# State-space preparation in another order: rotation tables before output matrices, first four table pairs ahead of the kernel copies

## What is computed

```python
dt = exp(log_dt); a_bar = exp(lam * dt)              # 32 groups, 64 complex states each
b_bar = ((a_bar - 1.0) / lam)[..., None] * b
bu = einsum('bsgc,gpc->bsgp', u, b_bar)
states = scan over positions of s = a_bar * s + bu   # complex, diagonal
y = einsum('bsgp,gcp->bsgc', states, c).real + d_skip * u
```

## Time and profile before

| | |
|---|---|
| median of 3 runs | 3012.65 us (3012.24 to 3018.19) |
| profiled execution | 3006.3 us |
| its span | 3004.5 us |
| PE busy | 2803.8 us, 93% of the span |
| DVE busy | 1913.6 us, 64% |
| ACT busy | 1357.6 us, 45% |
| POOL busy | 936.6 us, 31% |

### The profile page before, as it was taken

One profiled execution on the slowest core, in us unless ns is written; L12 is line 12 of the kernel. 1 busy time (PEld: TensorE's weight loads), 2 busy tenths in 40 slices (PEclk: granted clock), 3 DMA queues, 4 the chain that ended last, 5 costly groups with the idle time before them and its releaser, 6 DMA issues. The chain is left out here.

```text
span 3004.5 us, 43240 instructions
## 1 busy us (share of the span) xinstructions
PE 2803.8 (93%) x14883; PEld 2367.3 (79%) x14883; DVE 1913.6 (64%) x2803; ACT 1357.6 (45%) x2268; POOL 936.6 (31%) x743
## 2 busy tenths in 40 slices
PE   6999967879999998997899989999999999999999
PEld 5888854669899897886788778887888787878777
DVE  5334338768778786545667675657555868686864
ACT  4222224657667675322344455556555424242321
POOL 0011100745455552320000032333323344444443
PEclk9999988989999999998999999999999999999999
DMA  5333345263422203344132334333544374756555
GB/s 169 92 87 81 99 125 71 55 189 72 95 57 57 61 22 102 105 147 161 36 119 105 117 104 136 103 108 130 179 139 140 102 167 100 170 95 154 119 111 88
DMA packets 296004, 328.21 MB, mean 109 GB/s; under 512 B 114584, under 2 KB 221088, under 8 KB 295584
## 3 DMA queue, kind: packets, MB, share of 16 engines
q1 hardware_dynamic: 276960, 291.96, 32.7%
q0 software_dynamic: 18432, 33.56, 7.9%
q10 hardware_dynamic: 464, 0.79, 0.1%
HBM read 206.57 MB, written 126.88 MB: 111 GB/s over the span
## 5 line engine op out<-in xcount | busy, mean ns | idle before, releaser
L3235 PE MATMUL f_ps_bank<-f_big,h_wv 128*128 128x512 f32 x1280 | 503.1, 393 | 25.6 <-DVE f_big L3081 20.3
L3236 PE MATMUL f_ps_bank<-f_big,h_wv 128*128 128x512 f32 x1280 | 500.0, 391 | 0.0
L3237 PE MATMUL f_ps_bank<-f_big,h_wv 128*128 128x512 f32 x1280 | 500.0, 391 | 0.0
L704 POOL TENSOR_TENSOR a_w<-a_on,a_left 128x640 f32<-128x640 f32 (+5 forms) x192 | 282.1, 1469 | 243.3 <-DVE a_left L756 108.9
L3077 DVE TENSOR_TENSOR h_wv<-h_w_raw,h_wv 128x512 fp32r<-128x512 f32 x189 | 241.9, 1280 | 155.1 <-ACT h_wv L2978 151.7
L2978 ACT ACTIVATE h_wv<-h_w_sum 128x512 fp32r<-128x512 f32 x252 | 158.9, 631 | 349.7 <-PE f_ps_bank L3237 342.2
L2919 POOL TENSOR_TENSOR h_w_sum<-h_w_raw 128x512 f32<-128x512 f32 x63 | 91.2, 1447 | 721.6 <-DMA h_w_raw<-in_w_up 441.8
L3235 PEld LDWEIGHTS f_ps_bank<-f_big,h_wv 128*128 128x128 f32 x1280 | 241.5, 189 | 83.5 <-issue 28.8
L3237 PEld LDWEIGHTS f_ps_bank<-f_big,h_wv 128*128 128x128 f32 x1280 | 241.4, 189 | 50.7
L3236 PEld LDWEIGHTS f_ps_bank<-f_big,h_wv 128*128 128x128 f32 x1280 | 241.7, 189 | 49.5
L846 PE MATMUL a_ps_y<-a_wt,a_v 128*96 128x128 f32 x2176 | 269.9, 273 | 3.3 <-DVE a_yt L779 3.3
(11 more groups left out here) (400 smaller groups left out, 6211.2 us busy)
## 6 DMA issues: line engine op xcount, KB each, us to landing
h_w_raw<-in_w_up SPq DMA_DIRECT2D x32, 1024.0 KB, 6.7
a<-h_xr SPq DMA_DIRECT2D x128, 256.0 KB, 3.4
h_w_raw<-a SPq DMA_DIRECT2D x32, 1024.0 KB, 5.1
out<-h_xr POOLq DMA_DIRECT2D x128, 256.0 KB, 4.0
h_raw<-in_w_down SPq DMA_DIRECT2D x32, 512.0 KB, 6.5
p_xt<-in_x SPq DMA_DIRECT2D x16, 512.0 KB, 4.5
p_raw<-in_w_in SPq DMA_DIRECT2D x16, 512.0 KB, 5.4
q<-p_raw SPq DMA_DIRECT2D x64, 128.0 KB, 2.5
```

Of the source, the lines that this page charges most:

```text
L704: pool.tensor_tensor(w[m % WS][:, 0:k1 - k0], on[m % ONS][:, 0:k1 - k0], left[a][i % 2][:, at + k0 + 1:at + k1 + 1], ALU.mult).then_inc(we ...
L3235: pe.matmul(o, wv(i, 0)[:, k, :], hv(i, 0)[:, k, :], start=(k == 0), stop=False)
L3236: pe.matmul(o, wv(i, 0)[:, k, :], hv(i, 1)[:, k, :], start=False, stop=False)
L3237: mm = pe.matmul(o, wv(i, 1)[:, k, :], hv(i, 0)[:, k, :], start=False, stop=(k == KH - 1))
```

## The change

On DVE the block of the output matrices is moved behind the low tables. On ACT, `parts` for pairs 0 to 3 is moved from behind the copies of the kernel and of `mat_out_j` to ahead of both. No instruction is added or taken away, apart from where they wait; the loops of PE, POOL and SP are as they were.

```diff
@@ ACT
             for n in range(G // 4):
                 copy_in(n)
+            act.wait_ge(low_ready, 1)
+            for p in range(4):
+                parts(p, 0)
+                parts(p, 1)
             for n in range(G // 4):
                 act.wait_ge(kern_made, n + 1)
                 act.activation(kern[:, 4 * n:4 * n + 4, :], y_ps[n % 2][0:C, :].rearrange("p (g s) -> p g s", g=4),
...
                                ACT.Copy).then_inc(crossed_copied, 1)
-            act.wait_ge(low_ready, 1)
-            for p in range(4):
-                parts(p, 0)
-                parts(p, 1)
             for p in range(1, PAIRS):
@@ DVE
             dve.sem_inc(keys_scaled, 1)
 
-            dve.wait_ge(in_rows, 1)
-            c_of = [cc[:, x, :].rearrange("p (g c) -> p g c", c=C) for x in range(2)]
-            above = pw[:, 1:SUB + 1, :, :]
-            both(dve.tensor_copy(mat_out[:, :, 0, :], c_of[0]),
-                 dve.tensor_tensor(mat_out[:, :, 1:, :], by_row(c_of[0]), by_power(above, 0), ALU.mult),
-                 dve.tensor_tensor(wide4, by_row(c_of[1]), by_power(above, 1), ALU.mult))
-            dve.tensor_tensor(mat_out[:, :, 1:, :], mat_out[:, :, 1:, :], wide4, ALU.add).then_inc(out_rows, 1)
-
             def normalise(v, n, shape):
...
-            dve.wait_ge(out_rows, 1)
             both(dve.tensor_copy(turn8[:, 0, :], num[:, 9, :]), dve.tensor_copy(turn8[:, 1, :], num[:, 6, :]))
...
             dve.engine_nop().then_inc(low_ready, 1)
+
+            dve.wait_ge(in_rows, 1)
+            c_of = [cc[:, x, :].rearrange("p (g c) -> p g c", c=C) for x in range(2)]
+            above = pw[:, 1:SUB + 1, :, :]
+            both(dve.tensor_copy(mat_out[:, :, 0, :], c_of[0]),
+                 dve.tensor_tensor(mat_out[:, :, 1:, :], by_row(c_of[0]), by_power(above, 0), ALU.mult),
+                 dve.tensor_tensor(wide4, by_row(c_of[1]), by_power(above, 1), ALU.mult))
+            dve.tensor_tensor(mat_out[:, :, 1:, :], mat_out[:, :, 1:, :], wide4, ALU.add).then_inc(out_rows, 1)
+            dve.wait_ge(out_rows, 1)
```

## The result

| | before | changed |
|---|---|---|
| median of 5 runs | 3012.65 us | 3028.89 us |
| lowest, highest | 3009.95, 3018.19 | 3026.34, 3032.20 |
| ratio, 95% interval | | 1.0052 (1.0041 to 1.0062) |
| profiled execution, its span | 3006.3, 3004.5 | 3028.89, 3027.1 |

The changed kernel is 16.2 us slower. The forecast was 18.3 us, 3031.0 us in a range of 3023 to 3037.

The account below looks back on a forecast made before the run. The stage's pairs were taken to bound the kernel's end, with the DMAs becoming the first output's last need: first copy of y 17.7 us later plus 0.6 us restart slip, +18.3 us, median 3031.0 us, range 3023 to 3037.

Parts of the forecast that it names:

- DVE's two blocks in the other order: DVE: low tables first give low_ready at 504.6; output matrices (out_rows) ready at 518.8 instead of 491.1.
- The four pairs: ACT's tables of pairs 0 to 3 ahead of the kernel copies, held by POOL's rotate(0); parts(3, 1) ends at 532.9.
- the added wait: ACT's kernel copies queue behind parts(3, 1); PE stands after two steps, and the last copy ends at 539.5 against 512.08.
- POOL shut out: POOL's grow(0, 0) waits through DVE's first two big products until 513.5; the third product then runs 514.4 to 518.8.
- the sum: Total: first copy of y 17.7 us later plus 0.6 us at the restart, 18.3 us slower.
- The first rival: No blocking between POOL and DVE on the products' broadcast operands: +13.8, 3026.5 us; chance 0.11.
- The six remaining steps go at PE's pace, 0.89 us: PE's kernel steps after its stop: last kernel copy ends about 6.6 us after the first began.
- ACT's order sets the pace as now: Loop of pairs after the first copy of y: ACT's stream keeps the old pace, 5.09 us a pair.
- The slip at the restart: PE makes v of pair 3 before y of pair 1: 0.6 us allowed, between -0.4 and 1.3.
- a rival for it: The pairs catch up at DVE's and PE's pace, winning up to 6.6 us: +11.7, 3024.4 us; chance 0.05.

Follow-up runs that it names:

- halves_after: Changed kernel, with SP issuing the DMAs into mat_within in two halves, after four and after eight kernel copies; ratio to before 1.0035, stage +11.4 us.
- its counterpart: Kernel before, with the DMAs into mat_within split into the same two halves; ratio 0.9998, first output y(0) at 534.24.
- act_only: Kernel before with only ACT's stream changed (four pairs' tables ahead of the kernel copies), DVE's order old; ratio 1.0064, stage +21.5 us.
- two_ahead: Changed kernel, but ACT grows only the tables of pairs 0 and 1 ahead of the kernel copies; ratio to before 1.0017, stage +8.3 us.
- dve_only: Kernel before with only DVE's stream changed (low tables ahead of the output matrices), ACT's order old; ratio 1.0067, stage +16.8 us.

## Why the prediction was right

**Right, step by step.** DVE's two blocks in the other order: `out_rows` 518.99 on the clock of before, forecast 518.8. The low tables' first copies waited for the memset (2.44 us for two copies that take 0.27), as I had assumed; `low_ready` 505.0, forecast 504.6. The four pairs end at 528.70 + 1.70 + 2.38 = 532.8, forecast 532.9, and the kernel copies start there. The DMAs take from the last kernel copy (542.06) to y(0) (557.85) 15.8 us, forecast 15.7. That y(0) would be released by a DMA was right, and `halves_after` with its counterpart shows that it decides. `act_only` shows the added wait to be enough by itself; `two_ahead` shows its price at the first y to be one for one.

**Right in the end, wrong between.** I had POOL shut out until both first products were over. In fact each waited for one product and DVE for each in turn (3.26 and 4.63 us on POOL, 4.68 and 4.56 on DVE for 4.42). Either way the second join of pair 0 waits for the third product, so the sum is the same. The first rival, no blocking for broadcast operands, is refuted by these rows; the rule of the Trainium skill that the prediction names, on the ports that DVE and GpSimd share ("SBUF — State Buffer", section "Who interferes with whom"), holds for them too.

**Wrong terms of the sum, which cancel.** "The six remaining steps go at PE's pace, 0.89 us": from the first kernel copy to the end of the last I had 6.6 us, and it took 539.68 - 530.31 = 9.4. PE had stood for 11 us, its clock was granted at 0.50 from 530.9 to 536.0 and 0.98 afterwards (in the kernel before it was 1.00 for all eight steps):

```profile
530.90:536.00 5.10, 5.07 (x24) 3.58 (x25) 0.00 (x0) 1.63 (x3) 0.99 (x2) 0.50 0.00 0
536.00:549.10 13.10, 12.37 (x50) 6.21 (x47) 0.00 (x0) 8.59 (x17) 0.52 (x2) 0.98 0.46 58
```

The windows above are from the changed kernel. The third, fourth and fifth kernel copy start 1.7 us apart, the last ones 0.87, as before. It was a matter of reading: I took the mean of a stretch in which PE had just worked, for one in which it came from a stop. `make_y(0)` took 5.3 us instead of 4.7 for a like reason. Together 3.4 us too little; the copies began 0.2 us sooner than forecast, and with rounding that is the difference: the first copy of y came at 563.16, 20.8 us later and not 17.7.

On the other side "ACT's order sets the pace as now" was wrong. The slip at the restart was there (571.24 after 565.50, one round of 5.74), then the pairs came every 4.70 us instead of 5.13. From the first copy of y to the twelfth it took 52.7 us instead of 56.0: 3.3 us back, against the 0.6 us of slip in my sum. I had a rival for it with a chance of 0.05, that DVE's or PE's work takes over the pace. What let the pace change was something else: POOL's join no longer fell into DVE's rotation. Where it came to rest is closer to the rival than I had said, since PE is 97% busy at that pace. From the twelfth copy to the last it took 0.6 us more than before. So the end of the stage came 20.8 - 3.3 + 0.6 = 18.1 us later, the sum said 18.3, and the medians say 16.2 (12 to 19 by the interval). The direction and the chain were foreseen; that the total fits to 0.2 us is luck, two misses of 3 us in opposite directions.

**What stays open.** Why the start by DMA leads into one pattern of rounds and the start by rotation into the other was not tried by itself; that the eight kernels with the old order of rotations and copies of y divide in this way, five to three, is an observation. Nor was the blocking between POOL and DVE taken away by itself. That PE's own work is what holds a round near 4.7 us is read from its busy time; no run made that work shorter. In the changed kernel ACT's chain closes in 4.70 us as well, and the two are not told apart. Nor do the runs say why PE's clock fell in `dve_only` after a stop of 2.0 us.

## What to carry to other kernels

Work that is moved ahead of a copy on an in-order engine holds everything that the copy feeds: follow the copy to its last consumer, here through PE's eight steps and 15.7 us of DMAs, before calling a branch idle. Where two branches meet, a branch that gets ready 5 us sooner wins nothing if the other had 6.3 us of slack and comes 30 us later, as the DMAs did here (kernel copies done at 542.1 instead of 512.1). In a loop of engines in lockstep, look at the duration of one instruction over the rounds: where it is longer than alone, two engines meet, and one swap in an instruction stream can be worth more than a new order of the preparation.

## What was not expected of the hardware

PE's clock after a stop: 6.3 us idle and the next 5.3 us are granted 0.53; 2.8 us idle and the clock stays at 1.00, and the same products take 2.9 us. But the length of the stop does not decide alone: in `dve_only` the clock was 1.00 before and during a stop of 2.0 us and 0.61 in the 4.4 us after it, while in the kernel before it stayed at 1.00 through a stop of 1.9 us at the same place. And POOL and DVE, with two big DVE products and two small POOL joins queued, took turns, one instruction each, where the earlier trace rows had shown POOL waiting through two.
